# A hybrid attention layer on one Trainium2 core: one more pair of query tiles is searched beside attention

## The chip, the cores and the metric

The kernel runs on one core of a Trainium2 chip. The metric is the device time of one execution in microseconds (us). Every input and output lies in HBM; inside the core work runs on TensorE (PE, with its weight loads PEld), VectorE (DVE), ScalarE (ACT), GpSimd (POOL) and SyncE (SP, which issues all DMAs here). Each engine works through its own list of instructions in the order in which it was written, and waits at semaphores for the others.

## The reference

The layer takes 2048 tokens of width 1024, puts 16 meta tokens in front and computes

- `proj = h @ w_in`, split into queries, keys and values of branch A, queries and latents (`c_kv`) of branch B, the indexer's queries, key and head weights, and 2048 gate columns;
- branch A: chunk-causal sliding-window attention, 8 heads;
- branch B: for each query an index score over all visible keys, the sum over 8 heads of `w * relu(q_idx . k_idx)`; the best 256 keys are kept (`lax.top_k(score, 256)`), and attention runs over those alone;
- the gated sum of both branches, an output projection, a layer norm, a SwiGLU FFN and a second layer norm.

In float32, to float32 accuracy: products of the projection use three passes of a high and a low part (`matmul3`).

## The kernel before, in words

Queries are worked in 16 tiles of 128 rows (`TILES`); tile t sees `width(t) = 16 + 128 (t + 1)` keys, so tiles 12, 13, 14, 15 see 1680, 1808, 1936 and 2064. The kernel is four blocks, each ending with all engines:

1. `ln`: layer norm and the first eight column chunks of the projection.
2. `se` (the "second block"): in steps n = -39 to 106, three kinds of work side by side. (a) The rest of the projection: 96 units (a chunk of 128 columns for a group of 512 tokens), each of 8 *pieces*, a piece being one `matmul3` of 512 columns, three matmuls. (b) Index scores, one head of one tile in each step: step n has head m = n + 32, tile m // 8 (`IDX_AHEAD`). TensorE makes them (`index`, L845/L846; it runs two steps ahead), ScalarE rectifies them into three buffers (`rectify`, L920), VectorE adds them up (`sum_index`, L1033). (c) The search for the 256th largest score of a pair of tiles q = (2q, 2q+1), by bisection in 31 rounds (`ROUNDS`), and then the selection. The search of the even tile counts on VectorE (`tally`, L1054), that of the odd one on ScalarE (`tally`, L941/L943/L945: from round 9 on ScalarE makes the next candidate itself); GpSimd decides between rounds (`judge`). Two rounds of each go into a step. The even tile of pair q + 1 is searched in steps 16q - 8 to 16q + 7, the odd one in 16q to 16q + 15. Then each tile is selected in eight steps (`select`: `restore`, `mark_above`, `mark_equal`, `number_equal`, `choose`, `join`, `mask`) and its distances are stored in HBM (`distances`, `store_distances`). Pairs 0 to 6 (tiles 0 to 13, `LATE = 7`) are done so; tiles 12 and 13 are searched in steps 72 to 95 and selected in steps 88 to 103.
3. `at` (attention): one head of one tile per step, n = 0 to 127, tile n // 8. TensorE makes logits (L102 to L104), transposes (L1597, L1630) and weighs (L1619); VectorE adds distances to the logits (L1832); ScalarE takes exponentials (L1704, L1712) and copies transposed blocks out (L1724). Pair 7 (tiles 14 and 15), whose index scores stay in SBUF (`late_score`), is searched here, one round per step, in steps 56 to 89 (`search`, `LATE_STEP`): VectorE L1947, ScalarE L1764/L1766/L1768, GpSimd L1478. Tiles 14 and 15 are selected in steps 104 to 119, straight into the distance buffer.
4. `ff`: gates, output projection, FFN.

How many pieces of the projection a step of the second block takes is planned by `piece_steps`: it spreads them by an estimate of each step's other work (`columns`), never more than 8 in a step, and pauses for three steps where the second half of the token groups is swapped in (`RELOAD_STEPS`). The plan of before gives 8 pieces to each step from 55 to 102 (4 to 8 to most steps from 8 to 51), pauses at 52 to 54, and puts none at 103 to 106. Steps 96 to 102 hold 56 pieces and no index score: the last index score is added at step 95.

On every engine the order within a step is written out. TensorE's is: first block of the index score, half of the pieces, the other blocks, the other pieces. `index` waits until ScalarE has emptied the bank that it writes (two banks); `rectify` waits for VectorE to have used a buffer (`rel_free`).

The attention's search puts its work at the end of each engine's step:

```
def search(n):                       # of ScalarE, before
    r = n - LATE_STEP - 1
    if r == -1: orient()
    if r == 0: flip()
    if 0 <= r < ROUNDS: tally(r)
```

Of the kernel before, what the change touches and what calls it, by code (L numbers as in the profile page):

```python
# [62 lines left out]
LATE = TILES // 2 - 1  # L63
LATE_STEP = 7 * HEADS
FIRST_STEP, LAST_STEP = -IDX_AHEAD - 7, HEADS * (2 * LATE - 2) + 10
# [117 lines left out]
def project_and_select(nc, x, meta_tokens, ln0_g, ln0_b, w_in, b_gate, kv_norm_g, k_idx_g, k_idx_b, h0, proj, v_nat, h_kept, c_kept, dist_kept, late_score, w_uk, wuk_t):  # L183
# [6 lines left out]
    with Scope(nc, "pj") as s:  # L190
# [18 lines left out]
        with Scope(nc, "ln") as a:  # L209
            xt = [a.sb(f"x{u}", [P, D]) for u in range(2)]  # L210
            spare = [late_score[:, c // 2, c % 2 * D:c % 2 * D + D].rearrange("p (k c) -> p k c", k=KT) for c in range(4)]
            raws = [t[:, :, :] for t in raw] + spare + [a.sb(f"raw{c}", [P, KT, P])[:, :, :] for c in range(6, len(FIRST_CHUNKS))]
# [9 lines left out]
            part = [a.sb(f"part{v}", [P, GROUP]) for v in range(3)]  # L222
# [247 lines left out]
        with Scope(nc, "se") as a:  # L470
# [15 lines left out]
            score = [a.sb("score0", [P, 2, L - 2 * P]), late_score]  # L486
# [66 lines left out]
            with nc.Block() as block:  # L553
# [92 lines left out]
                def _(pool):  # L646
# [120 lines left out]
                    def part_b(n, half):  # L767
                        q, r = search_b(n, half)
                        if n >= 0 and n % (2 * HEADS) == 0 and half == 0 and n:
# [431 lines left out]
def attention(nc, proj, v_nat, wuk_t, w_uv, sinks, attn, c_kept, dist_kept, score):  # L1201
# [4 lines left out]
    with Scope(nc, "at") as s:  # L1206
# [22 lines left out]
        kth, fix_count, fix_cand = s.sb("kth", [P, 2]), s.sb("fix_count", [P, 1]), s.sb("fix_cand", [P, 1])  # L1229
# [80 lines left out]
        def late(t):  # L1310
            return score[:, t % 2, 0:width(t)]
# [7 lines left out]
        with nc.Block() as block:  # L1319
# [70 lines left out]
            def _(pool):  # L1390
# [42 lines left out]
                def orient(c):  # L1433
                    w = width(2 * LATE + c)
                    pool.wait_ge(count_ready[c], 1 + START)
# [14 lines left out]
                def judge(c, r):  # L1450
                    if c and len(EXPONENTS) < r < ROUNDS - 1:
                        return
                    pool.wait_ge(count_ready[c], 2 + r + START)
# [16 lines left out]
                    elif c:  # L1470
# [4 lines left out]
                        pool.tensor_tensor(one(kth, c), one(cand, c), one(step, c), ALU.add)  # L1475
                    else:
# [8 lines left out]
                        else:  # L1485
                            pool.tensor_tensor(one(kth, c), one(base, c), one(step, c), ALU.add)
                    pool.drain()

                def settle_a():
                    pool.tensor_scalar(one(undo, 0), one(sign, 0), 1.0, None, ALU.mult)  # L1490
                    pool.tensor_tensor(one(kth, 0), one(kth, 0), one(sign, 0), ALU.mult)
# [3 lines left out]
                def settle_first():  # L1495
                    pool.tensor_scalar(one(undo, 1), one(sign, 1), 1.0, None, ALU.mult)
                    pool.tensor_scalar(one(kth, 1), one(kth, 1), -1.0, None, ALU.mult)
                    pool.drain()
                    pool.tensor_tensor(fix_cand[:, :], one(kth, 1), steps[:, 1, MANTISSA - 1:MANTISSA], ALU.subtract).then_inc(fix_ready, 1)
                    w = width(2 * LATE + 1)  # L1500
# [3 lines left out]
                def settle_second():  # L1504
                    pool.wait_ge(fix_counted, 1 + START)
                    pool.tensor_scalar(one(step, 1), fix_count[:, :], one(wanted, 1), steps[:, 1, MANTISSA - 1:MANTISSA], ALU.is_ge, ALU.mult)
                    pool.drain()
                    pool.tensor_tensor(one(kth, 1), one(kth, 1), one(step, 1), ALU.subtract)
                    pool.drain()
                    pool.tensor_tensor(one(kth, 1), one(kth, 1), one(sign, 1), ALU.mult).then_inc(kth_ready[1], 1)  # L1510
                    pool.drain()

                def search(n):

                    r = n - LATE_STEP - 1
                    if r == -1:
                        orient(0)
                        orient(1)
                    if 0 <= r < ROUNDS:
                        judge(0, r)  # L1520
                        judge(1, r)
                    if r == ROUNDS - 1:
                        settle_a()
                        settle_first()
                    if r == ROUNDS + 1:
                        settle_second()
# [168 lines left out]
            def _(act):  # L1695
# [51 lines left out]
                def orient():  # L1747
                    t = 2 * LATE + 1
                    act.activation(junk_s[:, 0:width(t)], late(t), ACT.Sign, accum_out=one(count, 1)).then_inc(count_ready[1], 1)

                def flip():
                    t = 2 * LATE + 1
                    act.wait_ge(sign_ready[1], 1 + START)
# [3 lines left out]
                def tally(r):  # L1757

                    t, i = 2 * LATE + 1, r - len(EXPONENTS) - 1
                    if i <= 0:  # L1760
                        act.wait_ge(cand_ready[1], r + 1 + START)
# [8 lines left out]
                def search(n):  # L1770

                    r = n - LATE_STEP - 1
# [4 lines left out]
                    if 0 <= r < ROUNDS:  # L1777
                        tally(r)
# [39 lines left out]
            def _(dve):  # L1818
# [52 lines left out]
                def restore(t):  # L1871
                    c, x = t % 2, late(t)
                    dve.wait_ge(kth_ready[c], 1 + START)
                    dve.tensor_scalar(x, x, one(undo, c), None, ALU.mult)
                    dve.drain()

                def mark_above(t):
                    c, w, x = t % 2, width(t), late(t)
                    dve.tensor_scalar(greater[:, 0:w], x, one(kth, c), None, ALU.is_gt, ALU.add, accum_out=one(above, c))
                    dve.drain()  # L1880

                def mark_equal(t):
                    c, w, x = t % 2, width(t), late(t)
                    dve.tensor_scalar(equal[:, 0:w], x, one(kth, c), None, ALU.is_equal)
# [50 lines left out]
                def orient():  # L1935
                    t = 2 * LATE
                    dve.tensor_scalar(junk_v[:, 0:width(t)], late(t), 0.0, None, ALU.is_ge, ALU.add, accum_out=one(count, 0)).then_inc(count_ready[0], 1)

                def flip():
                    dve.wait_ge(sign_ready[0], 1 + START)  # L1940
                    dve.tensor_scalar(late(2 * LATE), late(2 * LATE), one(sign, 0), None, ALU.mult)
# [656 lines left out]
```

## Time and profile before

| | us |
|---|---|
| median of 3 runs | 4093.33 |
| lowest and highest | 4085.76, 4095.21 |
| the profiled execution | 4090.23 |
| its span, first to last instruction | 4088.1 |

| stretch of the span (us) | what runs |
|---|---|
| 0 to about 263 | first block |
| about 263 to 1209 | second block (last piece at 1205) |
| 1209 to about 2140 | attention |
| 2140 to 4088 | mixing and FFN |

In the span TensorE is busy 3731.0 us (91%), VectorE 1617.5 (40%), ScalarE 1777.7 (43%), GpSimd 1627.7 (40%). A busy TensorE counts modelled ends of matmuls that overlap; what it waits for is seen in the idle time before an instruction. The column PEclk is the clock that TensorE was granted, as a share of 2.4 GHz; it has two levels, 1.2 and 2.4 GHz.

### The profile page before, as it was taken

What the parts mean: (1) busy time and instruction counts of PE and PEld (TensorE: products, weight loads), DVE (VectorE), ACT (ScalarE), POOL (GpSimd) and SP (SyncE); (2) the same over time, 40 slices, a digit from 0 to 9 for tenths busy, and PEclk for the clock granted to TensorE, in tenths of its full rate; (3) what the DMA queues carried; (4) which work ended last, traced back from release to release, by engine and by line L of the source; (5) the groups of instructions that cost most, each with busy time, mean ns of one, the idle gap of its engine ahead of it and who ended that gap; (6) DMA issues with size and microseconds to landing.
All of it is one profiled execution on the core that took longest, in us unless ns stands there. A gap on an engine that the chain in (4) does not pass through costs nothing. (4 is left out here: it accounts for less than half of the span.)

```text
span 4088.1 us, 53536 instructions
## 1 busy us (share of the span) xinstructions
PE 3731.0 (91%) x18658; PEld 3092.7 (76%) x18658; DVE 1617.5 (40%) x2432; ACT 1777.7 (43%) x3161; POOL 1627.7 (40%) x1743
## 2 busy tenths in 40 slices
PE   5997788788889999999998989799999999999997
PEld 4875556566667888999986777688878878887886
DVE  4216666788732236634524665311131031113102
ACT  3213677778843668865542222222222222222221
POOL 5213566666521112110014555344444444444443
PEclk9988899899996999999998999899999999999999
DMA  7323322422231111110006565233333333333332
GB/s 232 141 73 94 81 65 64 154 64 85 64 108 39 44 44 31 43 35 23 15 10 203 201 204 182 67 108 97 135 113 97 124 103 114 98 138 112 94 98 83
DMA packets 421781, 396.38 MB, mean 97 GB/s; under 512 B 20424, under 2 KB 361624, under 8 KB 418232
## 3 DMA queue, kind: packets, MB, share of 16 engines
q1 hardware_dynamic: 410048, 342.28, 27.4%
q10 hardware_dynamic: 11520, 51.38, 3.4%
q8 instruction: 119, 1.95, 0.2%
q14 instruction: 94, 0.77, 0.1%
HBM read 302.51 MB, written 91.08 MB: 96 GB/s over the span
## 5 line engine op out<-in xcount | busy, mean ns | idle before, releaser
L2149 POOL TENSOR_TENSOR ff_w_lo<-ff_raw,ff_w_hi 128x1024 fp32r<-128x1024 f32 x328 | 787.0, 2400 | 958.3 <-ACT ff_w_hi L2187 958.3
L2187 ACT ACTIVATE ff_w_hi<-ff_raw 128x1024 fp32r<-128x1024 f32 x328 | 346.0, 1056 | 854.8 <-PE ff_bank L104 739.1
L102 PE MATMUL ff_bank<-ff_h_hi,ff_w_lo 128*128 128x512 f32 x1408 | 551.2, 392 | 16.3 <-POOL ff_w_lo L2149 10.3
L103 PE MATMUL ff_bank<-ff_h_hi,ff_w_hi 128*128 128x512 f32 x1408 | 550.0, 391 | 0.0
L104 PE MATMUL ff_bank<-ff_h_lo,ff_w_hi 128*128 128x512 f32 x1408 | 550.0, 391 | 0.0
L102 PE MATMUL ff_bank<-ff_w_hi,ff_f 128*128 128x512 f32 x960 | 373.9, 389 | 4.6 <-DVE ff_mixed L2434 4.3
L104 PE MATMUL ff_bank<-ff_w_lo,ff_f 128*128 128x512 f32 x960 | 373.5, 389 | 0.0
L103 PE MATMUL ff_bank<-ff_w_hi,ff_f 128*128 128x512 f32 x960 | 373.5, 389 | 0.0
L1619 PE MATMUL at_ctx<-at_p_t,at_c_nat 128*128 128x128 f32 (+1 forms) x2432 | 351.5, 285 | 7.9 <-ACT at_ctx_t L1730 7.0
L1619 PEld LDWEIGHTS at_ctx<-at_p_t,at_c_nat 128*128 128x128 f32 (+1 forms) x2432 | 306.1, 194 | 37.7 <-ACT at_ctx_t L1730 13.2
L1724 ACT ACTIVATE at_p_t<-at_turn 128x512 f32<-128x512 f32 (+4 forms) x416 | 214.2, 544 | 266.3 <-PE at_turn L1597 226.4
L102 PEld LDWEIGHTS ff_bank<-ff_h_hi,ff_w_lo 128*128 128x128 f32 x1408 | 265.7, 189 | 75.0 <-issue 20.2
L103 PEld LDWEIGHTS ff_bank<-ff_h_hi,ff_w_hi 128*128 128x128 f32 x1408 | 265.9, 189 | 55.3
L104 PEld LDWEIGHTS ff_bank<-ff_h_lo,ff_w_hi 128*128 128x128 f32 x1408 | 265.6, 189 | 55.7
L845 PE MATMUL se_big_i<-se_ki_hi,se_qi 128*128 128x512 f32 (+16 forms) x392 | 149.7, 382 | 155.2 <-ACT se_rel L920 154.1
L2285 ACT ACTIVATE ff_f<-ff_mixed 128x512 f32 (+1 forms) x88 | 55.6, 632 | 437.3 <-DVE ff_mixed L2434 437.3
L845 PEld LDWEIGHTS se_big_i<-se_ki_hi,se_qi 128*128 128x128 f32 x392 | 79.3, 202 | 217.6 <-ACT se_rel L920 187.6
L102 PEld LDWEIGHTS ff_bank<-ff_w_hi,ff_f 128*128 128x128 f32 x960 | 180.2, 188 | 43.9 <-issue 6.6
L104 PEld LDWEIGHTS ff_bank<-ff_w_lo,ff_f 128*128 128x128 f32 x960 | 180.2, 188 | 37.6
L103 PEld LDWEIGHTS ff_bank<-ff_w_hi,ff_f 128*128 128x128 f32 x960 | 180.2, 188 | 37.2
L920 ACT ACTIVATE se_rel<-se_big_i 128x272 f32<-128x272 f32 (+14 forms) x248 | 155.5, 632 | 90.5 <-DVE late_score L1033 47.8
L1832 DVE CUSTOM_DVE_ANT_0 at_u_b<-at_big_l,at_dist 128x528 f32<-128x528 f32 (+11 forms) x128 | 106.8, 834 | 207.9 <-PE at_big_l L104 198.8
(350 smaller groups left out, 7740.8 us busy)
## 6 DMA issues: line engine op xcount, KB each, us to landing
ff_raw<-in_w_ff_gate SPq DMA_DIRECT2D x88, 512.0 KB, 3.8
ff_raw<-in_w_ff_up SPq DMA_DIRECT2D x88, 512.0 KB, 3.8
ff_raw<-in_w_ff_down SPq DMA_DIRECT2D x88, 512.0 KB, 3.5
pj_raw<-in_w_in SPq DMA_DIRECT2D x50, 512.0 KB, 4.6
proj<-se_row SPq DMA_DIRECT2D x96, 256.0 KB, 2.2
ff_f<-proj SPq DMA_DIRECT2D x64, 256.0 KB, 3.5
ff_raw<-in_w_out SPq DMA_DIRECT2D x32, 512.0 KB, 3.5
ln_x<-in_x SPq DMA_DIRECT2D x16, 512.0 KB, 4.9
```

The lines of the kernel that those rows point to most:

```text
L102: pe.matmul(out, lhs_lo, rhs_hi, start=start, stop=False)
L103: pe.matmul(out, lhs_hi, rhs_hi, start=False, stop=False)
L104: return pe.matmul(out, lhs_hi, rhs_lo, start=False, stop=stop)
L845: pe.matmul(big_i[i % 2][:, a:a + n], qi_2[t % 2][:, h, :], ki_hi[:, cols], start=True, stop=False)
L920: act.activation(rel[i % RELS][:, 0:wb], big_i[i % 2][:, 0:wb], ACT.Relu).then_inc(rel_ready, 1)
L1619: last = pe.matmul(ctx[:, 0, :], c_nat[0:rows, a:a + P], p_t[v][0:rows, m, :], start=(a == 0), stop=(a + rows == w))
L1724: act.activation(p_t[v][0:rows, 0:many, :], turn[u][0:rows, 0:many * P].rearrange("p (m q) -> p m q", m=many), ACT.Copy).then_inc(turn_fre ...
L1832: dve.tensor_tensor_reduce(u_b[n % 3][:, a0:a0 + wb], big_l[i % 2][:, 0:wb], dist[t % 2][:, a0:a0 + wb], 2.0 ** -(h + 1), min_b[:, c, b - ...
L2149: pool.tensor_tensor(w_lo[u][:, :], raw[u][:, :], f32(w_hi[u][:, :]), ALU.subtract).then_inc(lo_ready[u], 1)
L2187: act.activation(w_hi[u][:, :], raw[u][:, :], ACT.Copy).then_inc(hi_ready[u], 1)
L2285: act.activation(piece(f_hi, 2 * i + n), feature[:, :], ACT.Copy).then_inc(feat_hi, 1)
```

## The change

`LATE` goes from 7 to 6: the second block searches and selects tiles 0 to 11 only. The scores of tiles 12 and 13 stay in SBUF too (`late_score` is now both score buffers, and some scratch of the first block is laid into them), and the attention block has two searches: pair 6 from step 37, pair 7 from step 71 (it was 56). Tiles 12 and 13 are selected in attention's steps 88 to 103, with pair 7's search running. Attention loads distances for tiles 0 to 11 only. The counts write to scratch tiles of their own (`junk_v`, `junk_s`) instead of `greater` and `equal`.

The second block ends at step 97 instead of 106. `piece_steps` is unchanged but gives another plan: the 56 pieces of steps 96 to 102 go to earlier steps, 45 more to steps -32 to 39 and 11 more to steps 40 to 55; the pause is at steps 45 to 47 instead of 52 to 54; steps 56 to 95 hold 8 pieces each as before.

```diff
-LATE = TILES // 2 - 1
-LATE_STEP = 7 * HEADS
-FIRST_STEP, LAST_STEP = -IDX_AHEAD - 7, HEADS * (2 * LATE - 2) + 10
+LATE = TILES // 2 - 2
+LATE_STEPS = {LATE: 37, LATE + 1: 71}
+FIRST_STEP, LAST_STEP = -IDX_AHEAD - 7, max(HEADS * (2 * LATE - 2) + 10, STEPS - IDX_AHEAD + 1)
...
-            score = [a.sb("score0", [P, 2, L - 2 * P]), late_score]
+            score = late_score
...
-        junk_v, junk_s = greater, equal
-        undo = s.sb("undo", [P, 2])
+        junk_v, junk_s = s.sb("junk_v", [P, L], BF16), s.sb("junk_s", [P, L], BF16)
+        undo = s.sb("undo", [P, 4])
...
         def late(t):
-            return score[:, t % 2, 0:width(t)]
+            return score[t // 2 % 2][:, t % 2, 0:width(t)]
+
+        def late_round(n):
+
+            for q, first in LATE_STEPS.items():
+                if first <= n <= first + ROUNDS + 2:
+                    return q, n - first - 1
+            return None, None
+
+        def nth(q, many):
+
+            return (q - LATE) * many + START
...
                 def search(n):
 
-                    r = n - LATE_STEP - 1
+                    q, r = late_round(n)
                     if r == -1:
-                        orient()
+                        orient(q)
                     if r == 0:
-                        flip()
-                    if 0 <= r < ROUNDS:
-                        tally(r)
+                        flip(q)
+                    if q and 0 <= r < ROUNDS:
+                        tally(q, r)
...
-        late_score = s.sb("score", [P, 2, L])
+        late_score = [s.sb("score0", [P, 2, L - 2 * P]), s.sb("score1", [P, 2, L])]
```

The other hunks carry the pair q through `orient`, `flip`, `tally`, `judge`, `settle_*` and `restore` of the three engines, with semaphore counts and thresholds (`kth`, `undo`) for both pairs.

## Rows read from the trace of the kernel before

**Rows 1.** The page's head and its part 1, busy time of each engine.

```profile
span 4088.1 us, 53536 instructions
PE 3731.0 (91%) x18658; PEld 3092.7 (76%) x18658; DVE 1617.5 (40%) x2432; ACT 1777.7 (43%) x3161; POOL 1627.7 (40%) x1743
```

**Rows 2.** Windows, second block: length, PE, PEld, DVE, ACT, POOL busy, PEclk, DMA, GB/s.

```profile
625.00:683.00 58.00, 50.62 (x209) 38.86 (x208) 37.25 (x61) 42.69 (x75) 39.12 (x89) 0.91 0.24 70
683.00:744.00 61.00, 52.10 (x231) 40.28 (x230) 50.67 (x67) 47.28 (x86) 36.47 (x72) 0.98 0.30 81
744.00:808.00 64.00, 45.76 (x172) 34.92 (x172) 48.58 (x61) 49.88 (x78) 42.54 (x86) 0.78 0.56 194
808.00:873.00 65.00, 57.99 (x258) 45.62 (x257) 55.50 (x64) 51.39 (x86) 39.77 (x66) 1.00 0.25 75
...
945.00:1021.00 76.00, 61.97 (x260) 47.20 (x259) 66.20 (x65) 59.60 (x90) 47.57 (x75) 1.00 0.26 72
1021.00:1105.00 84.00, 68.83 (x265) 53.68 (x264) 64.89 (x65) 64.17 (x84) 53.68 (x91) 0.90 0.23 66
1105.00:1167.00 62.00, 58.10 (x262) 46.78 (x262) 32.91 (x33) 55.63 (x87) 15.68 (x22) 1.00 0.23 74
1167.00:1206.00 39.00, 38.93 (x167) 31.02 (x165) 15.85 (x12) 6.52 (x10) 13.98 (x13) 1.00 0.24 85
```

**Rows 3.** Waits of TensorE, 1021 to 1105 us: total us, times, longest.

```profile
PE se_big_i L845 <- ACT se_rel L920: 15.2, 8, 3.9
```

**Rows 4.** Waits of TensorE, 1105 to 1167 us.

```profile
PE se_big_i L845 <- ACT se_rel L920: 3.9, 6, 1.1
```

**Rows 5.** Groups by line, VectorE, 942 to 1105 us: busy, mean ns, idle before.

```profile
L1054 DVE TENSOR_SCALAR_CACHE_REDUCE se_junk_v<-se_score,se_cand 128x1680 bf16<-128x1680 f32 x31 | 60.8, 1962 | 20.8 <-POOL se_cand L726 15.5 <-POOL se_cand L703 2.4 <-POOL se_cand L714 1.7
```

**Rows 6.** Groups by line, ScalarE, 1019 to 1167 us.

```profile
L945 ACT ACTIVATE se_junk_s<-se_score,se_cand 128x1808 bf16<-128x1808 f32 x31 | 55.9, 1803 | 15.4 <-POOL se_cand L703 9.7 <-POOL se_cand L714 4.1
...
L943 ACT ACTIVATE se_cand<-se_verdict,se_cand,se_steps 128x1 f32<-128x1 f32 x22 | 8.5, 387 | 1.8 <-issue 0.3
L941 ACT ACTIVATE se_verdict<-se_count,se_limit 128x1 f32<-128x1 f32 x22 | 6.5, 295 | 1.8
```

**Rows 7.** Windows, attention: the columns of rows 2, eight steps in each stretch.

```profile
1393.00:1434.00 41.00, 40.71 (x301) 35.69 (x303) 13.40 (x26) 25.52 (x68) 6.86 (x7) 1.00 0.16 46
1434.00:1478.00 44.00, 43.84 (x323) 38.97 (x321) 14.47 (x26) 26.94 (x67) 6.58 (x7) 1.00 0.15 44
1478.00:1527.00 49.00, 48.84 (x361) 43.62 (x360) 17.68 (x34) 30.83 (x71) 6.75 (x14) 1.00 0.14 41
1527.00:1583.00 56.00, 55.10 (x407) 48.31 (x406) 36.66 (x59) 48.59 (x93) 16.39 (x42) 1.00 0.12 37
1583.00:1642.00 59.00, 58.75 (x442) 52.90 (x442) 36.53 (x58) 52.73 (x105) 14.99 (x37) 1.00 0.12 37
1642.00:1704.00 62.00, 61.86 (x469) 56.22 (x469) 37.65 (x58) 55.49 (x108) 12.59 (x30) 1.00 0.12 36
1704.00:1770.00 66.00, 65.89 (x502) 60.09 (x501) 39.40 (x59) 54.61 (x106) 15.29 (x39) 1.00 0.11 35
1770.00:1839.00 69.00, 68.27 (x515) 62.55 (x514) 22.49 (x43) 38.40 (x83) 6.62 (x6) 1.00 0.11 34
```

**Rows 8.** Timeline of ScalarE, 1601 to 1605 us, one round: start, us.

```profile
1601.61 0.29 ACT L1764 ACTIVATE at_verdict<-at_count,at_limit 128x1 f32<-128x1 f32 x1
1601.97 0.39 ACT L1766 ACTIVATE at_cand<-at_verdict,at_cand,at_steps 128x1 f32<-128x1 f32 x1
1602.42 2.02 ACT L1768 ACTIVATE at_equal<-late_score,at_cand 128x2064 bf16<-128x2064 f32 x1
...
1604.44 1.06 ACT L1724 ACTIVATE at_p_t<-at_turn 128x512 f32<-128x512 f32 x2
```

**Rows 9.** Groups by line, VectorE, 1478 to 2080 us.

```profile
L1947 DVE TENSOR_SCALAR_CACHE_REDUCE at_greater<-late_score,at_cand 128x1936 bf16<-128x1936 f32 x31 | 69.0, 2225 | 2.5 <-issue 2.4
...
L1890 DVE TENSOR_TENSOR_SCAN late_score<-at_equal 128x1936 f32<-128x1936 bf16 (+1 forms) x2 | 8.6, 4314 | 0.0
```

More of the change, by code:

```diff
@@ L221, in project_and_select @@
             rstd = [a.sb(f"rstd{u}", [P, 1]) for u in range(2)]
-            part = [a.sb(f"part{v}", [P, GROUP]) for v in range(3)]
+            part = [late_score[0][:, c, D:D + GROUP] for c in range(2)] + [wuk_t[:, :, :].rearrange("p j c -> p (j c)")]
             zeros = part[0]
@@ L768, in part_b @@
                         q, r = search_b(n, half)
-                        if n >= 0 and n % (2 * HEADS) == 0 and half == 0 and n:
+                        if n > 0 and n % (2 * HEADS) == 0 and half == 0 and n // (2 * HEADS) < LATE:
                             settle_second(n // (2 * HEADS))
@@ L1474, in judge @@
                         pool.drain()
-                        pool.tensor_tensor(one(kth, c), one(cand, c), one(step, c), ALU.add)
+                        pool.tensor_tensor(one(kth, k_of(c, q)), one(cand, c), one(step, c), ALU.add)
                     else:
@@ L1485, in judge, with settle_a @@
                         else:
-                            pool.tensor_tensor(one(kth, c), one(base, c), one(step, c), ALU.add)
+                            pool.tensor_tensor(one(kth, k_of(c, q)), one(base, c), one(step, c), ALU.add)
                     pool.drain()
-                def settle_a():
-                    pool.tensor_scalar(one(undo, 0), one(sign, 0), 1.0, None, ALU.mult)
-                    pool.tensor_tensor(one(kth, 0), one(kth, 0), one(sign, 0), ALU.mult)
+                def settle_a(q):
+                    pool.tensor_scalar(one(undo, k_of(0, q)), one(sign, 0), 1.0, None, ALU.mult)
+                    pool.tensor_tensor(one(kth, k_of(0, q)), one(kth, k_of(0, q)), one(sign, 0), ALU.mult)
@@ L1878, in mark_above @@
                     c, w, x = t % 2, width(t), late(t)
-                    dve.tensor_scalar(greater[:, 0:w], x, one(kth, c), None, ALU.is_gt, ALU.add, accum_out=one(above, c))
+                    dve.tensor_scalar(greater[:, 0:w], x, one(kth, k_of(c, t // 2)), None, ALU.is_gt, ALU.add, accum_out=one(above, c))
                     dve.drain()
@@ L1933, in distances, with orient, flip @@
                     dve.drain()
-                def orient():
-                    t = 2 * LATE
+                def orient(q):
+                    t = 2 * q
                     dve.tensor_scalar(junk_v[:, 0:width(t)], late(t), 0.0, None, ALU.is_ge, ALU.add, accum_out=one(count, 0)).then_inc(count_ready[0], 1)
-                def flip():
-                    dve.wait_ge(sign_ready[0], 1 + START)
-                    dve.tensor_scalar(late(2 * LATE), late(2 * LATE), one(sign, 0), None, ALU.mult)
+                def flip(q):
+                    dve.wait_ge(sign_ready[0], 1 + nth(q, 1))
+                    dve.tensor_scalar(late(2 * q), late(2 * q), one(sign, 0), None, ALU.mult)
@@ L1942, in flip, with tally, tally_fix @@
                     dve.drain()
[L1944 to L1946 removed]
+                def tally(q, r):
+                    t = 2 * q
+                    dve.wait_ge(cand_ready[0], r + 1 + nth(q, ROUNDS))
                     dve.tensor_scalar(junk_v[:, 0:width(t)], late(t), one(cand, 0), None, ALU.is_ge, ALU.add,
                                       accum_out=one(count, 0)).then_inc(count_ready[0], 1)
[L1950 to L1953 removed]
+                def tally_fix(q):
+                    t = 2 * q + 1
+                    dve.wait_ge(fix_ready, 1 + nth(q, 1))
+                    dve.tensor_scalar(junk_v[:, 0:width(t)], late(t), fix_cand[:, :], None, ALU.is_ge, ALU.add,
@@ L1954, in tally_fix @@
                                       accum_out=fix_count[:, :]).then_inc(fix_counted, 1)
                 def search(n):
-                    r, (t, h) = n - LATE_STEP - 1, divmod(n, HEADS)
+                    (q, r), (t, h) = late_round(n), divmod(n, HEADS)
                     if r == -1:
-                        orient()
+                        orient(q)
                     if r == 0:
-                        flip()
-                    if 0 <= r < ROUNDS:
-                        tally(r)
+                        flip(q)
@@ L1965, in search @@
+                    if q and 0 <= r < ROUNDS:
+                        tally(q, r)
                     if r == ROUNDS:
-                        tally_fix()
+                        tally_fix(q)
                     if t + 1 >= 2 * LATE and t + 1 < TILES:
```

83 lines of the change are left out of this document (39 added, 44 removed).

## The prediction, made before the changed kernel was run

> **What bounds the kernel now.** I read the page's part 1 first: TensorE is busy 91% of the span, VectorE, ScalarE and GpSimd 40 to 43% [rows 1]. But that is an average over four blocks, and the change touches two of them, which the windows tell apart. In the second block I cut the span wherever TensorE had done the pieces of eight more steps of the plan, so a row of that table is eight steps [rows 2]. In the last row (steps 96 to 102, projection alone) TensorE is busy 38.93 of 39 us: 167 matmuls, 0.233 us each, so a piece of three costs 0.70 us and 56 pieces 39.2 us. In the rows before it TensorE has slack: 61.97 of 76 us busy in steps 72 to 79, 68.83 of 84 in steps 80 to 87, then 58.10 of 62 in steps 88 to 95. The difference between these three is the search: two searches run in the first two, only ScalarE's in the third. TensorE's waits say the same: in the 84 us it stood 15.2 us until ScalarE had emptied an index bank, in the 62 us only 3.9 [rows 3, 4]. ScalarE and VectorE come late with the index score because a round of the search stands before it in their lists.
>
> In attention the same columns look different [rows 7]: TensorE is busy 40.7 of 41 to 68.3 of 69 us in every row, at PEclk 1.00. This block is bound by TensorE's own work, and the search of pair 7 (steps 56 to 89, from the fourth row on) lies beside it. ScalarE there is busy 48.59 of 56, 52.73 of 59 and 55.49 of 62: 87 to 90%.
>
> **The change, part by part.** The sum is against the profiled execution's 4090.2 us (its span 4088.1 and 2.1 around it); the median of the runs is 3.1 us more.
>
> *The tail goes.* Steps 96 to 102 disappear from the end of the block. VectorE's share there (selection of tile 13) is hidden anyway; what the path loses is the 39.2 us of pieces: **-39**. What follows the last piece (copy out, store, end of block) stays.
>
> *Steps 80 to 95 without search.* TensorE's own work in a step is 8 pieces, 5.6 us, and the index score. With 512 columns in 0.233 us (0.455 ns a column) and two passes over the keys this is 2 x 1936 x 0.455 = 1.76 us for tile 14 and 1.88 for tile 15. TensorE is two steps ahead, so steps 80 to 87 hold six heads of tile 14 and two of tile 15: 44.8 + 14.3 = 59.1 us. Now 84. VectorE loses 16 rounds of 1.96 us [rows 5], ScalarE 16 of about 2.7 (1.80 + 0.39 + 0.30 and the reading of the sum) [rows 6]. What is left for VectorE is adding and selecting tile 11, far under 59. I add 1.5 us of waits: 60.6, **-23**. Steps 88 to 95 hold the last six heads of tile 15: 44.8 + 11.3 = 56.1; with 1 us of waits 57, now 62: **-5**.
>
> *Steps 72 to 79 without VectorE's search.* ScalarE's search of pair 5 stays. The row to compare is steps 88 to 95 of before, which has just that: 62 us for 56.1 of TensorE's work, 5.7 more. TensorE's work here is 44.8 + six heads of tile 13 (1.65 each) + two of tile 14 = 58.2; plus 5.7 is 63.9, now 76: **-12**.
>
> *The 56 pieces moved forward.* As work of TensorE they cost 39.2 us, in steps where TensorE has idle time. Bounds: 0 and +39. The nearest rows are steps 32 to 63: 48, 55, 36 and 64 pieces take 58, 61, 64 and 65 us [rows 2]. The row with 20 to 28 pieces fewer than its neighbours is no shorter than the line between them (63), so up to there a row is set by the search and index chain, and a piece is nearly free. The pause for the reload is in that row too, so it is not a clean proof. I take **+6**: some pieces will stand before an index score that ScalarE is ready for.
>
> A row that bears on the clock: the stretch with the pause was granted 0.78 of 2.4 GHz, that is it partly ran at the 1.2 GHz level, after TensorE had been without pieces; the dense rows around it got 0.98 and 1.00 [rows 2]. "TensorE: Matmul & The Clock Gate" of the Trainium skill (Part 1) says that the throttled state is the default and that activity releases it. By that rule the denser steps would run no slower, but a TensorE that waits on ScalarE in attention could fall to the lower level; no attention row shows this (1.00 with ScalarE at 90%).
>
> *Attention: pair 7's search moves from step 56 to 71.* Its rows there have more TensorE work per step (62 us and up per eight steps) and ScalarE at most at 90%: it becomes slightly better hidden. The rows grow by 3, 5, 7, 3, 3, 4, 3 us; the 7 where pair 7's search begins suggests that it cost 2 to 3 us. Half of it goes: **-1**.
>
> *Attention: pair 6's search in steps 37 to 70.* On ScalarE a round of pair 7 occupies 2.83 us from its first instruction to the next work [rows 8]. For 1808 columns instead of 2064 it is 0.21 less (1.803 against 2.016), 2.62; the first rounds have no verdict and candidate (0.81) and take 1.81. In steps 40 to 47: 26.94 + 7 x 1.81 + 2.62 = 42.2 us of work in a row of 44. In steps 48 to 55: 30.83 less the 2.1 of pair 7's first count, plus 8 x 2.62 = 49.7 us in a row of 49: **ScalarE is full there**. In steps 56 to 63, 30.8 (on the line between 26.94 and 38.40) + 21.0 = 51.8 of 55. So for some 16 steps TensorE will wait. If ScalarE reaches 95% of its time, the rows become 44.5 and 52.5: +0.5 and +3.5; the start (first count, sign flip and two rounds within steps 37 to 39, 41 us row) another +2; steps 56 to 70 +1. Sum **+7**. Bounds: 0 if all of it is hidden as at 90%, and +80 if none is: 31 x 1.99 + 22 x 0.68 + 4 us for count and flip is what ScalarE gets in addition.
>
> *VectorE in attention.* Pair 6's counts fall into rows where it is busy a third of the time. In steps 88 to 103 a step can hold a count (2.2) and the scan (4.3 at 1936 columns) [rows 9] beside its 2.7 of other work: up to 9.4 us against steps of 7.8 to 9, for two steps in a row. Its logits are two steps ahead of their use, so a lag of 3 us is covered: **+1**, up to +8 if not.
>
> *At no cost:* separate scratch for the counts, scores in other addresses (same shapes), two distance tiles fewer to store and load (DMA idle, nobody waits), semaphore arithmetic. GpSimd's rounds run once per step and wait for counts.
>
> Sum: -39 - 23 - 5 - 12 + 6 - 1 + 7 + 1 = -66; 4090.2 - 66 = **4024 us**.
>
> **Rivals.** (A) *All hidden*: the moved pieces and attention's search cost 0 to 2: 4090 - 79 = 4011. For it: the 36-piece row, and the 90% rows. Against: steps 48 to 55. (B) *The moved pieces are paid in full*: +33 on the forecast, 4057. For it: TensorE's list is in order, each piece delays the index score behind it. Against: 36 pieces took as long as 55. (C) *ScalarE becomes the bound of attention from step 37 to 63*, not only where its sum exceeds the row: transposes, copies and exponentials go back and forth between the two engines, and a tally between them costs half of its length in 26 rounds, 26 x 2.4 / 2 = 31 instead of 7: 4048. (D) *Slower*: the same place, but ScalarE's 80 us stand wholly in series with TensorE: 4024 - 7 + 80 = 4097. It decides from the point where at least 75 of the 80 us show up; in the 90% rows 3 or fewer of 80 did. (E) *Steps 72 to 95 don't speed up*, because the adding chain (rectify, three buffers, VectorE) bounds them rather than the rounds: 20 of the 40 us lost, 4044. Against: the 62 us row has the same adding and little waiting. (F) *The change doesn't do what it says*: if the searches' counts met late thresholds, GpSimd would stall selection; there is no sign of that, price unknown, around 4090.
>
> **How the numbers follow.** Forecast 55%, A 15%, B 8%, C 11%, E 6%, D 3%, F 2%. The forecast's own range is 4014 to 4034. Eight in ten need A and most of C and E: 4006 to 4049. A measurement here tells about 0.2% (8 us) from no change. Slower is D alone, 3%; same is F, 2%; faster 95%.
>
> **What would show it.** In the second block: the last piece at about 1205 - 73 = 1132 us; steps 72 to 95 in 182 us instead of 222; steps -32 to 55 as long as before within 10 us. If these grow by 30, B. In attention: rows of steps 40 to 55 longer by 4 us together with ScalarE over 93% busy; rows 88 to 103 unchanged; PEclk 1.00. C shows as rows 37 to 63 longer by 25 or more with ScalarE, not TensorE, without idle time. The prediction is wrong if steps 80 to 87 stay above 68 us, or if attention as a whole grows by over 20.

## The result and the profile after

| | before | changed |
|---|---|---|
| median of 4 runs, us | 4092.82 | 4016.35 |
| lowest and highest | 4085.76, 4095.21 | 4012.19, 4023.9 |
| the profiled execution, us (its span) | 4090.23 (4088.1) | 4023.9 (4021.7) |
| ratio of the changed kernel to before | | 0.9818, 95% interval [0.9807, 0.9829] |

The change takes 76 us off the median. The forecast was 4024, with 4006 to 4049 as its range. The profiled execution is the longest of the four, so the profile shows 66 of the 76 us.

The windows of the second block, cut again where TensorE had done the pieces of eight more steps (columns as in [rows 2]). The first four are steps 32 to 63, the last three steps 72 to 95, which are now the end of the block:

```profile
629.00:690.00 61.00, 53.82 (x238) 42.92 (x236) 41.00 (x63) 45.53 (x80) 41.78 (x92) 0.96 0.31 89
690.00:748.00 58.00, 42.56 (x182) 34.32 (x181) 48.22 (x63) 45.75 (x84) 37.70 (x71) 0.84 0.65 226
748.00:811.00 63.00, 59.64 (x259) 47.65 (x259) 49.42 (x63) 49.36 (x78) 41.89 (x86) 0.96 0.23 62
811.00:876.00 65.00, 58.45 (x259) 45.73 (x258) 55.28 (x66) 52.07 (x89) 43.62 (x74) 1.00 0.27 76
946.00:1010.00 64.00, 60.05 (x260) 47.61 (x259) 31.51 (x31) 58.59 (x90) 21.27 (x27) 1.00 0.29 84
1010.00:1069.00 59.00, 59.00 (x265) 48.40 (x263) 38.44 (x33) 25.75 (x32) 20.40 (x17) 1.00 0.34 108
1069.00:1125.00 56.00, 56.00 (x261) 46.00 (x260) 17.23 (x19) 20.66 (x29) 10.53 (x12) 1.00 0.14 48
```

Steps 72 to 95 took 76, 84 and 62 us [rows 2] and take 64, 59 and 56. In the last two TensorE is never idle, and the waits for ScalarE of [rows 3, 4] are gone; in steps 72 to 79, where ScalarE still searches pair 5, they are small:

```profile
PE se_big_i L845 <- ACT se_rel L920: 4.0, 5, 0.8
```

Step 72 begins at 946 us, as before (945), although 56 more pieces have been done by then. Step 40 begins 7 us later than before, and what lies between gives 6 us back. The last piece is issued at 1124.9 instead of 1205.1 us.

The same windows in attention, eight steps each, from step 32 to step 63 and from 88 to 103. Against [rows 7], which end with step 95, the first three (41, 44 and 49 us there) and that of steps 88 to 95 (69) have grown:

```profile
1311.00:1355.00 44.00, 42.13 (x299) 36.78 (x298) 22.32 (x35) 33.22 (x77) 11.83 (x27) 0.96 0.15 43
1355.00:1401.00 46.00, 44.85 (x329) 39.52 (x327) 29.59 (x42) 41.68 (x88) 17.10 (x44) 1.00 0.14 42
1401.00:1453.00 52.00, 49.81 (x364) 43.68 (x366) 30.72 (x48) 48.13 (x101) 12.61 (x30) 1.00 0.13 39
1453.00:1509.00 56.00, 54.82 (x404) 47.84 (x400) 33.47 (x58) 49.91 (x107) 12.61 (x30) 1.00 0.13 37
...
1695.00:1767.00 72.00, 69.62 (x517) 63.12 (x517) 54.11 (x71) 59.49 (x115) 19.96 (x30) 1.00 0.07 20
1767.00:1841.00 74.00, 72.61 (x540) 66.64 (x539) 53.35 (x69) 56.34 (x107) 22.49 (x36) 1.00 0.07 19
```

ScalarE is busy 48.13 of 52 us in steps 48 to 55, 93%, and TensorE is no longer busy throughout: 49.81 of 52. More finely, by ScalarE's copies of the context (one in each step), the stretches of 40.9, 44.2 and 49.4 us became 44.3, 45.4 and 52.1, and those of 69.4 and 73.1 us became 71.7 and 74.2. From the first of these copies to that of step 120 attention took 836.8 us and takes 846.7. A second profiled execution of the changed kernel took 848.6; the 1.9 us between the two lie in steps 8 to 15, long before the search. What follows took 2017.1 us from there to the end of the span and takes 2021.8, with the same code; that is unevenness between executions (2012.2 to 2022.8 us in all the profiled executions of this document). So -81.0 before attention, +9.9 in it and +4.7 behind it are the -66.4 of the span.

### The profile page after: what moved, and what is told of

The parts are those of the page before. It is cut to its first block and busy times, and to the rows that moved or that the text cites. A ratio compares the mean times of both kernels' runs of the same rounds, so it can differ in the third digit from the quotient of the medians.

```text
span 4021.7 us, 53531 instructions
## 1 busy us (share of the span) xinstructions
PE 3706.1 (92%) x18658; PEld 3080.0 (77%) x18658; DVE 1620.2 (40%) x2432; ACT 1772.5 (44%) x3161; POOL 1611.5 (40%) x1743
## 5 line engine op out<-in xcount | busy, mean ns | idle before, releaser
L2299 ACT ACTIVATE ff_f<-ff_mixed 128x512 f32 (+1 forms) x88 | 55.6, 632 | 438.8 <-DVE ff_mixed L2448 438.8
L1054 DVE TENSOR_SCALAR_CACHE_REDUCE se_junk_v<-late_score,se_cand 128x400 bf16<-128x400 f32 (+4 forms) x155 | 180.2, 1162 | 124.4 <-POOL se_cand L726 97.8
L1033 DVE SCALAR_TENSOR_TENSOR late_score<-se_rel,se_w_idx,late_score 128x272 f32<-128x272 f32 (+14 forms) x217 | 194.9, 898 | 73.1 <-ACT se_rel L920 66.1
L945 ACT ACTIVATE se_junk_s<-late_score,se_cand 128x528 bf16<-128x528 f32 (+4 forms) x155 | 180.2, 1163 | 66.5 <-POOL se_cand L703 41.5
```

The lines of the kernel that those rows point to most:

```text
L945: act.activation(junk_s[:, 0:width(t)], score_of(t), ACT.Sign, bias=one(cand, 1), accum_out=one(count, 1)).then_inc(count_ready[1], 1)
L1033: dve.scalar_tensor_tensor(out=out, in0=rel[i % RELS][:, 0:wb], scalar=w_idx[:, t, h:h + 1], in1=out, op0=ALU.mult, op1=ALU.add).then_inc( ...
L1054: dve.tensor_scalar(junk_v[:, 0:width(t)], score_of(t), one(cand, 0), None, ALU.is_ge, ALU.add, accum_out=one(count, 0)).then_inc(count_re ...
L2299: act.activation(piece(f_hi, 2 * i + n), feature[:, :], ACT.Copy).then_inc(feat_hi, 1)
```

## The experiments

Kernels with a ratio were timed in turn with the kernel before on one chip; two (without ScalarE's rounds of pair 6, without VectorE's rounds of pair 7) ran once only, with a profile, and have none. In the tables "attention" is from the context copy of step 0 to that of step 120 in the profiled execution, and the stretches are measured between such copies too.

### One part at a time: the plan of pieces, and the search

The search moved, the pieces planned as before:

```diff
-FIRST_STEP, LAST_STEP = -IDX_AHEAD - 7, max(HEADS * (2 * LATE - 2) + 10, STEPS - IDX_AHEAD + 1)
+FIRST_STEP, LAST_STEP = -IDX_AHEAD - 7, HEADS * (2 * (LATE + 1) - 2) + 10
...
-        tally = 2 * width(2 * q + 2) + 600 if 0 <= q < LATE - 1 else 0
-        chosen = [1, 2, 1, 2, 1, 1, 1, 0][h] * width(t + 1) if 0 < t < 2 * LATE - 1 else 0
+        tally = 2 * width(2 * q + 2) + 600 if 0 <= q < LATE else 0
+        chosen = [1, 2, 1, 2, 1, 1, 1, 0][h] * width(t + 1) if 0 < t < 2 * LATE + 1 else 0
```

> The changed kernel with the plan of pieces of the kernel before: 56 pieces in steps 96 to 102 again, the pause at steps 52 to 54. Everything else as changed. Theory: the tail of 39 us comes back, and the 1 to 6 us that the moved pieces cost go: 35 to 38 us slower than the changed kernel, about 4053, ratio to before 0.990; last piece about 40 us earlier than before the change. Rival (a piece moved is paid where it goes, in full or half): the plan is worth less than 20 us, ratio under 0.987.

And the kernel before with the new plan alone:

```diff
-def piece_steps():
+def piece_steps(LATE=TILES // 2 - 2, LAST_STEP=STEPS - IDX_AHEAD + 1):
```

> The kernel before with the new plan of pieces alone; pair 6 is searched and selected in the second block as before. Theory: steps up to 71 take as long as before within 2 us, steps 72 to 95 stay at 222 us, and the tail holds only the selection of tile 13 on VectorE (about 16 us of work) and the storing of its distances: some 20 us of the 39 are gained, about 4073, ratio 0.995. So the change is worth more than its parts, because each part empties the tail only halfway. Rival (the plan gives its whole 39 us by itself): 4054, ratio 0.990. Other rival (pieces paid in full where they go): 4092 or more.

| | ratio to before, 95% | step 40 begins | step 56 | step 72 | last piece | attention's first copy |
|---|---|---|---|---|---|---|
| before | 1 | 682.9 | 808.1 | 945.2 | 1205.1 | 1234.2 |
| new plan only | 0.9937 [0.9921, 0.9954] | 690.5 | 810.8 | 946.7 | 1162.1 | 1208.9 |
| search moved, old plan | 0.9913 [0.9897, 0.9930] | 683.7 | 809.2 | 946.1 | 1163.3 | 1191.6 |
| both (the change) | 0.9818 [0.9807, 0.9829] | 690.1 | 810.4 | 946.3 | 1124.9 | 1153.2 |

In the sum the moved pieces cost next to nothing: with either plan step 72 begins within 0.2 us of the other where the search of pair 6 has gone, within 1.5 where it has not. They are not free where they go, though. The new plan has 45 more of them before step 40, and step 40 begins 6.4 to 7.6 us later with it. That is 0.14 to 0.17 us for each, where a piece alone takes 0.70. Between steps 40 and 72, with 11 more, 6.1 to 6.2 us come back. The plans differ there in the place of the pause too: steps 48 to 55 took 64.2 and 64.4 us with 36 pieces and the pause, 62.7 (twice) with 64 pieces and no pause; steps 40 to 47 took 61.1 us (twice) with 55 pieces, 57.7 (twice) with 38 pieces and the pause. No run moves the pause alone. Of the theories, full or half payment falls; the plan is worth 38.4 us at attention's start. With the search moved and the old plan the tail is back, TensorE alone, and the stretches before it are as short as in the changed kernel. Columns as in [rows 2]:

```profile
1009.00:1068.00 59.00, 59.00 (x264) 48.41 (x263) 39.24 (x33) 25.59 (x32) 26.89 (x20) 1.00 0.30 91
1068.00:1125.00 57.00, 57.00 (x266) 46.77 (x265) 17.22 (x19) 21.86 (x31) 13.35 (x16) 1.00 0.23 69
1125.00:1164.00 39.00, 39.00 (x168) 31.21 (x166) 0.00 (x0) 6.66 (x9) 5.63 (x8) 1.00 0.18 61
```

The new plan alone gives 25 us at attention's start, where 20 was expected: the last piece comes 43 us earlier, but attention starts 47 us after it instead of 29, because the selection of tile 13 now stands there with nothing beside it. This is the timeline of VectorE there (start, us), with the last piece issued at 1162.1:

```profile
1163.77 1.16 DVE L1066 TENSOR_SCALAR se_score<-se_score,se_undo 128x1808 f32<-128x1808 f32 x1 [1.18 <-POOL se_kth L755]
...
1168.51 3.93 DVE L1082 TENSOR_TENSOR_SCAN se_score<-se_equal 128x1808 f32<-128x1808 bf16 x1
...
1176.80 2.04 DVE L1147 SCALAR_TENSOR_TENSOR se_dist<-se_query_key,se_equal 128x1808 f32<-128x1808 f32 x1
```

One thing came otherwise than expected: steps 72 to 95 did not stay at 222 us but took 216 (73, 81 and 62), which is why the last piece comes 43 us earlier and not 39. No run shows why.

25.3 and 42.6 us add to 67.9; together they bring 81.0. The tail held two things side by side, and only taking both out removes it.

### Pair 6's rounds taken out of attention

The first count, the flip and the rounds of pair 6 are left out, first on all three engines, then ScalarE's alone; and, for the last stretches, VectorE's rounds of pair 7. With `LEFT_OUT` as `[(6, 0), (6, 1)]`, `[(6, 1)]` and `[(7, 0)]` (pair, tile of the pair). The first hunk is ScalarE's, the second GpSimd's; VectorE's is like them, and the semaphore thresholds follow:

```diff
                     q, r = late_round(n)
+                    if (q, 1) in LEFT_OUT:
+                        return
                     if r == -1:
                         orient(q)
...
-                        orient(q, 0)
-                        orient(q, 1)
+                        for c in range(2):
+                            if (q, c) not in LEFT_OUT:
+                                orient(q, c)
```

> The changed kernel without the first count, the flip and the 31 rounds of pair 6 in attention, on VectorE, ScalarE and GpSimd (tiles 12 and 13 are still selected, against a threshold that was never searched). Theory (those rounds fill ScalarE in steps 37 to 63): the attention stretches of steps 32 to 55, 44.3, 45.4 and 52.1 us in the changed kernel, fall to about 41, 44 and 48; attention is shorter by 7 to 8 us and the whole by as much, about 4008 us, ratio to before 0.980. The stretches of steps 88 to 103 (71.7 and 74.2 us) stay, because selection and pair 7's rounds are still there. Rival (the growth of attention is an unevenness between executions, or comes from the scores' new addresses): stretches stay at 44, 45 and 52, ratio 0.982.

> The changed kernel without ScalarE's part of pair 6's rounds in attention (tile 13's search left out); VectorE's and GpSimd's rounds for tile 12 stay. Theory (ScalarE is what is full): steps 32 to 55 take about 41, 44 and 48 us as without any rounds. Rival (VectorE's count stands before the logits that TensorE and ScalarE wait for): they stay at 44, 45 and 52, or lose less than half of the excess of 7 us.

> The changed kernel without VectorE's part of pair 7's rounds (tile 14's search left out). Theory: steps 88 to 103 fall from 71.7 and 74.2 us to 69.5 and 73.1, as in the kernel before, since VectorE no longer falls behind in a tile's steps 1 to 3; steps 72 to 87 stay. Rival (ScalarE's rounds of pair 7 do it): they stay at 71.7 and 74.2.

| steps | 32-39 | 40-47 | 48-55 | 56-63 | 88-95 | 96-103 | attention |
|---|---|---|---|---|---|---|---|
| before | 40.9 | 44.2 | 49.4 | 55.6 | 69.4 | 73.1 | 836.8 |
| changed | 44.3 | 45.4 | 52.1 | 56.1 | 71.7 | 74.2 | 846.7 |
| the same, again | 44.3 | 45.4 | 52.1 | 56.1 | 71.7 | 74.1 | 848.6 |
| no rounds of pair 6 | 40.9 | 44.2 | 49.3 | 54.9 | 71.7 | 74.2 | 838.7 |
| none on ScalarE | 40.9 | 44.9 | 49.4 | 54.9 | 71.7 | 74.1 | 840.5 |
| none on VectorE, pair 7 | 42.7 | 45.4 | 52.1 | 56.1 | 70.3 | 73.2 | 841.7 |

The kernel without any rounds of pair 6 was timed: ratio 0.9805 [0.9788, 0.9821], which is not told apart from the changed kernel's 0.9818 (4014 us, where 4008 was expected); the stretches do tell. Their growth repeats to 0.1 us and vanishes with the rounds. Nearly all of it in steps 32 to 63 is ScalarE's: without its part, VectorE's counts cost 0.7 us in steps 40 to 47 and nothing elsewhere. One size was off: the rounds cost 8.6 us in the four stretches from step 32 to 63, and the start alone 3.4 of them, where I had put 2. In steps 88 to 103 the excess over before is 3.4 us, and 2.3 of it go with VectorE's rounds of pair 7; the expectation had all of it go.

ScalarE's timeline at the start (step 38 of the changed kernel; start, us) shows flip and first count back to back, 3.7 us, and the windows show what TensorE does meanwhile:

```profile
1339.16 1.81 ACT L1768 ACTIVATE late_score<-late_score,at_sign 128x1808 f32<-128x1808 f32 x1
1341.04 1.80 ACT L1782 ACTIVATE at_junk_s<-late_score,at_cand 128x1808 bf16<-128x1808 f32 x1
...
1342.84 0.58 ACT L1738 ACTIVATE at_p_t<-at_turn 128x512 f32<-128x512 f32 x1
```

```profile
1331.00:1339.00 8.00, 8.00 (x63) 7.38 (x63) 5.77 (x8) 7.78 (x21) 2.50 (x9) 1.00 0.01 3
1339.00:1347.00 8.00, 6.42 (x38) 5.67 (x37) 3.28 (x6) 7.93 (x13) 3.53 (x8) 0.80 0.00 0
```

TensorE waits 1.6 us, and in the same 8 us its granted clock is 0.80, that is partly at the 1.2 GHz level. "TensorE: Matmul & The Clock Gate" of the Trainium skill (Part 1) says that the throttled state is the default and that activity releases it. A fall right behind a wait agrees with that (0.80 here, 1.00 in the 8 us before); it is the fall that the prediction named and had not seen in [rows 7]. It goes with half of the excess of this stretch: the kernel without VectorE's rounds of pair 7 (table above) and the kernel with both edits (below) have the same wait in the same place and no fall, and take 42.7 us for it, not 44.3. So the two long instructions by themselves cost 1.8 us, close to the 2 of the forecast.

### An earlier start

```diff
-LATE_STEPS = {LATE: 37, LATE + 1: 71}
+LATE_STEPS = {LATE: 21, LATE + 1: 71}
```

> The changed kernel with pair 6's search started at attention's step 21 instead of 37, all else the same. Theory (a stretch is as long as the longer of TensorE's work and ScalarE's sum, which it fills to about 95%): ScalarE's sums are 20.4 + 5 rounds in steps 16 to 23 (hidden), 23.1 + 8 x 1.8 = 38 of 38.5 in steps 24 to 31, 25.4 + 8 x 2.6 = 46.4 against 41 in steps 32 to 39, 27.0 + 21 = 48 against 44 in steps 40 to 47, 29 + 7 x 2.6 = 47 against 49.3 in steps 48 to 55. At 95% that is 40, 49, 50.5 and 50: about 19 us over the stretches without rounds, where the start at 37 costs 8. So 10 to 12 us slower than the changed kernel, ratio 0.985 to 0.987. Rival (a round costs the same wherever it stands, 31 rounds for 8 us): no difference. Rival D (what exceeds comes wholly in series): 40 us and more slower.

Ratio 0.9855 [0.9831, 0.9880]; attention 862.9 us, 14 to 16 more than in the changed kernel. Windows from step 16 on, eight steps each:

```profile
1240.00:1283.00 43.00, 38.12 (x241) 32.89 (x239) 20.28 (x35) 29.35 (x71) 12.32 (x27) 0.88 0.14 40
1283.00:1325.00 42.00, 38.90 (x281) 32.62 (x278) 27.56 (x43) 37.87 (x89) 16.46 (x43) 1.00 0.15 43
1325.00:1371.00 46.00, 42.30 (x297) 36.60 (x297) 28.45 (x42) 43.53 (x98) 12.62 (x30) 0.96 0.15 41
1371.00:1420.00 49.00, 46.37 (x327) 40.51 (x325) 29.60 (x42) 46.23 (x101) 12.62 (x30) 0.97 0.14 39
```

The price depends on where the rounds stand, as expected, and neither rival holds: 31 rounds cost 23 us here (steps 16 to 63) and 9 there, not the same and not 40 more. The two stretches from step 32 came out under their sums (46.5 and 48.5 us measured, 49 and 50.5 expected), although each has a fall of the clock in it (0.96 and 0.97). ScalarE did fill them to 94 to 95%, as the theory said; its work was put 2 to 3 us too high. But steps 16 to 23, which should have hidden their five rounds, took 42.8 instead of 35.7 us with ScalarE at 68%: flip and first count fall into one short step there, and the clock of 0.88 over 43 us is by itself worth about 5 of the 7 us (an estimate: 0.12 x 43). An average over eight steps does not see one step that is too full.

### Less work on ScalarE, and VectorE's work spread

GpSimd makes the odd tile's next candidate in all rounds (the hunk is ScalarE's; GpSimd's `judge` gets three small instructions per round for it):

```diff
                 def tally(q, r):
...
-                    if i <= 0:
-                        act.wait_ge(cand_ready[1], r + 1 + nth(q, len(EXPONENTS) + 2))
-                    else:
-                        act.drain()
-                        act.activation(verdict[:, :], one(count, 1), ACT.Sign, bias=limit[:, :])
-                        act.drain()
-                        act.activation(one(cand, 1), verdict[:, :], ACT.Identity, scale=steps[:, 1, i:i + 1], bias=one(cand, 1))
-                        act.drain()
+                    act.wait_ge(cand_ready[1], r + 1 + nth(q, ROUNDS))
```

Selection starts one step earlier:

```diff
-                    if (at, half) == (1, 0):
-                        restore(t)
-                    if (at, half) == (1, 1):
-                        mark_above(t)
+                    if (at, half) == (7, 0) and t + 1 < TILES:
+                        restore(t + 1)
+                        mark_above(t + 1)
...
+                    if t + 1 == 2 * LATE - 1 and h == 7:
+                        select(t + 1, h, 0)
```

> The changed kernel as it is, once more, as the mark for the three kernels below on one chip: ratio to before 0.981 to 0.983; attention stretches of steps 32 to 55 near 44, 45 and 52 us, of steps 88 to 103 near 71.7 and 74.2 us.

> The changed kernel with ScalarE's two small instructions per round from round 9 on (verdict and candidate, 0.8 us of its time) given to GpSimd in attention. Theory (ScalarE's sum against the stretch is what makes steps 40 to 63 longer): ScalarE's load in steps 48 to 55 falls from 49.7 to about 43.5 us of 48, so that stretch falls from 52.1 to about 50, steps 56 to 63 from 56.1 to 55, steps 40 to 47 hardly (one such round there); 3 us in all. Rival C (each count stands between TensorE and ScalarE wherever the sum is): the stretches stay within 1 us, since the count of 1.8 us is unchanged. Other rival: GpSimd's answer comes too late for ScalarE's next count, and the stretches grow.

> The changed kernel with restore and mark_above of attention's selection moved from a tile's step 1 to step 7 of the tile before, where VectorE has nothing to select. Theory (in steps 88 to 103 VectorE falls behind at steps 1 to 3 of a tile, and TensorE waits for its low part of the absorbed query): the stretches 71.7 and 74.2 us fall to about 69.5 and 73.2, 3 us in all; the whole is 3 us faster, which these rounds hardly tell. Rival (pair 7's rounds on ScalarE make these stretches longer): they stay.

> Both edits together. Theory: the gains add, about 6 us under the changed kernel, ratio to before 0.980 to 0.981. Rival: what one stretch gives is lost in the next, ratio as that of the changed kernel.

In later runs, the flip in a step of its own as well:

```diff
-LATE_STEPS = {LATE: 37, LATE + 1: 71}
+LATE_STEPS = {LATE: 35, LATE + 1: 70}
...
-                    return q, n - first - 1
+                    return q, {0: -1, 1: -0.5}.get(n - first, n - first - 2)
...
-                    if r == 0:
+                    if r == -0.5:
                         flip(q)
```

> Both edits of the kernel before this one (selection spread, GpSimd's verdict), and the sign flip of a tile gets a step of its own before the first round, so that pair 6 starts at step 35 and pair 7 at 70. Theory (flip and first count together, 3.8 us of ScalarE in one step, make TensorE wait 1.6 us at step 39, and in some executions its clock falls to 1.2 GHz for a stretch after that wait): the stretch of steps 32 to 39 falls from 42.7 (without the fall) or 44.3 us (with it) to 41.5 or less, and no fall is seen in it. In the whole 1 to 2 us, which these rounds can't tell. Rival (what costs there is the answer of GpSimd that ScalarE waits for): the stretch stays at 42.7 or 44.3.

> The kernel with both edits (selection spread, GpSimd's verdict) once more, beside the one with the flip apart: ratio to before 0.980 to 0.982, 1 to 2 us more than that one, not told apart.

| | ratio to before, 95% | 32-39 | 40-47 | 48-55 | 56-63 | 88-95 | 96-103 | attention |
|---|---|---|---|---|---|---|---|---|
| changed, again | 0.9834 [0.9821, 0.9847] | 44.3 | 45.4 | 52.1 | 56.1 | 71.7 | 74.1 | 848.6 |
| selection spread | 0.9826 [0.9813, 0.9839] | 44.3 | 45.4 | 52.1 | 56.2 | 70.3 | 73.2 | 844.4 |
| GpSimd's verdict | 0.9821 [0.9808, 0.9834] | 44.3 | 45.4 | 49.6 | 54.9 | 70.9 | 74.2 | 843.6 |
| both | 0.9808 [0.9794, 0.9821] | 42.7 | 45.4 | 49.6 | 54.9 | 69.4 | 73.1 | 838.7 |
| both, second time | 0.9813 [0.9800, 0.9827] | 42.7 | 45.4 | 49.6 | 54.9 | 69.4 | 73.1 | 838.4 |
| both and flip apart | 0.9811 [0.9797, 0.9824] | 42.4 | 45.4 | 49.6 | 54.9 | 69.5 | 73.1 | 838.1 |

Taking 0.8 us from a round gives steps 48 to 55 back 2.5 of their 2.8 us, although the count of 1.8 us still stands where it stood: so it is the sum of ScalarE's work against the stretch that costs, not the place of the count (rival C). The window of steps 48 to 55 with GpSimd's verdict has TensorE busy throughout again and ScalarE at 86%:

```profile
1403.00:1453.00 50.00, 49.71 (x369) 44.05 (x369) 30.57 (x48) 43.00 (x87) 18.61 (x55) 1.00 0.14 40
```

Spreading the selection gives 2.3 us, the same as leaving VectorE's rounds of pair 7 out. GpSimd's verdict takes another 0.8 us out of steps 88 to 95, where pair 7's rounds lie on ScalarE too, and with both edits steps 88 to 103 are back at the 69.4 and 73.1 us of before. So the rival that blamed ScalarE's rounds of pair 7 holds for about a quarter of the 3.4 us. With both edits attention is as long as without pair 6's rounds at all (838.7). Than the changed kernel measured beside them, both edits are faster by 4024.1 - 4015.1 = 9 us; the intervals of the ratios only touch, but no run of the one reaches the other (4009.4 to 4016.3 against 4019.4 to 4025.8 us). The flip apart missed: 42.4 us instead of 41.5 or less. The burst is gone, but the very first count now falls into step 35, the tile's shortest, which takes 5.6 us instead of the 3.7 of before. No fall of the clock is seen there; as the kernel with both edits had none either, that says nothing for the flip. Its gain, if there is one, isn't told by the times.

## Why the prediction was right

The forecast of 4024 us was the profiled execution's own 4023.9, which is in part luck; against the median it was 8 us high, inside its own range of 4014 to 4034. Term by term:

| step of the sum | forecast | measured |
|---|---|---|
| tail of 56 pieces | -39 | -39 (1125 to 1164 in the old-plan kernel) |
| steps 80 to 87 | -23 | -25 |
| steps 88 to 95 | -5 | -6 |
| steps 72 to 79 | -12 | -12 |
| pieces moved forward | +6 | +1 |
| attention, rounds on ScalarE (less pair 7's move) | +6 | +7 |
| attention, VectorE in steps 88 to 103 | +1 | +3 |
| behind attention | 0 | +5 in this execution |

*The second block.* What let the three stretches be sized to 2 us was that TensorE's own work could be added up from two durations in a row where it was alone (0.233 us for 512 columns), and that a stretch with one search instead of two stood in the trace of before. The forecast of 63.9 us for steps 72 to 79 came from that stretch and met 64. Two small slips stand in the working and change nothing: 62 less 56.1 is 5.9 us and not 5.7, and the row of 36 pieces has 19 to 28 fewer than its neighbours, not 20 to 28.

*The moved pieces.* This is the mis-sized term: 6 us charged, 0.2 and 1.5 us measured between the two plans. The charge was about what the pieces cost up to step 40 (6.4 and 7.6 us); that the steps behind give it back was not in the sum. The row with 36 pieces, on which the idea of a free piece rested, was no fair witness: the same steps are 1.5 us shorter with 64 pieces and the pause elsewhere.

*Attention.* The place (steps 37 to 55, ScalarE full) and the sign were right, with 52.1 us measured for 52.5 forecast in steps 48 to 55. The start was under-sized: 3.4 us for 2, of which 1.6 go with the fall of the clock that the forecast had named and put at nothing. "PEclk 1.00", one of its signs, failed with that (0.96 over steps 32 to 39). So did "rows 88 to 103 unchanged": VectorE's lag was not covered as I had argued. Its low part of the absorbed query (`at_ql_lo`) came late for TensorE once in each of the two tiles. My check of the slack had looked at the logits alone. TensorE's weight loads in steps 88 to 103 of the changed kernel show the waits (total, times, longest); in the same stretches of the kernel with the selection spread there are none:

```profile
PEld at_misc L1568 <- DVE at_ql_lo L1854: 2.8, 2, 1.6
```

*The errors cancelled in part.* The second block gave 8 us more than forecast, attention cost 3 more, and the unchanged last block happened to be 5 longer in that execution. The sum met the profile to 0.1 us; the terms did not, and that they added up so well is luck.

Of the rivals, A (all hidden, 4011) was nearest to the median for half of a reason: the moved pieces cost 1 us in the sum, attention's rounds were not hidden. B and E are refuted by the windows, C by its own size (25 us or more in steps 37 to 63, measured 9) and by the kernel with GpSimd's verdict, D by attention's 10 us against 80, and F by the block that ended 80 us earlier.

## What to carry to other kernels

Where an in-order engine waits for others, more work of its own costs less than its length (45 pieces, 31 us of work, delayed step 40 by 6 to 8 us here): sum that work per stretch from a row in which it runs alone, and take the stretch's length against that. A tail that holds two kinds of work side by side pays only once both are gone (25 and 43 us apart, 81 together here). When work moves beside a saturated engine, add up the *helper's* time per step and not only per stretch: at 89 to 91% the rounds cost 1.2 us in stretches of 45 and 56, at 93% 2.8 us in 52, and two long instructions in one short step cost 1.8 us, or 3.4 with the fall of the clock.

## What the runs showed of the hardware

TensorE's granted clock fell to the 1.2 GHz level in attention after a single wait of 1.6 us in an otherwise full stretch, and not always. The kernel with both edits has the same instructions of ScalarE at that place and the same busy time of TensorE as the changed kernel, whose window is shown above (6.42 of 8 us, clock 0.80); its own window of the same 8 us:

```profile
1339.00:1347.00 8.00, 6.42 (x48) 5.66 (x47) 3.99 (x7) 7.93 (x14) 3.30 (x8) 1.00 0.00 0
```

The fall costs 1.6 us here. In the eight profiled executions with this start five had it (changed twice, old plan, selection spread, GpSimd's verdict) and three had not (without VectorE's rounds of pair 7, both edits twice). The wait alone does not decide. In the same five the clock had also fallen for a moment at step 18, long before the search, and in the three it had not, although TensorE's waits there (1.1 and 0.9 us) are the same in all of them and in the kernel before. The changed kernel, then the kernel with both edits:

```profile
1244.00:1252.00 8.00, 7.07 (x38) 5.56 (x36) 1.86 (x5) 4.25 (x14) 1.04 (x1) 0.79 0.33 90
```

```profile
1244.00:1252.00 8.00, 6.80 (x46) 5.60 (x47) 2.39 (x9) 3.75 (x12) 1.04 (x1) 1.00 0.33 90
```

Steps 16 to 23 took 36.8 to 36.9 us with that fall and 35.7 without. The kernel without ScalarE's rounds of pair 6 fell at step 18 too, and not at step 38, where it has no wait. The two kernels that were profiled twice did the same both times; what decides was not found out.

A longer fall stands at attention's start in every execution, and [rows 7] begin behind it, so "no attention row shows this" in the prediction holds for its own rows alone. In the kernel before, TensorE did nothing for 9 us between its last piece (1205) and attention's first work; the clock fell in that gap and stayed at the 1.2 GHz level until 1301; the first row is that kernel, the second the changed one:

```profile
1209.00:1301.00 92.00, 73.43 (x289) 59.80 (x290) 21.78 (x68) 27.32 (x89) 12.98 (x61) 0.50 0.24 71
```

```profile
1129.00:1204.00 75.00, 59.47 (x237) 48.79 (x238) 17.66 (x58) 21.26 (x70) 11.93 (x60) 0.50 0.27 78
```

How long it lasts differs between executions. In the other profiled execution of the changed kernel it lasted 92 us, as in the kernel before, and steps 8 to 15 took 39.7 us and not 37.9: that is the 1.9 us between the two.

A GpSimd instruction on one column took 1.02 us in the second block of the kernel before and 0.37 us in attention, in that kernel (0.367) as in the changed one (0.369), for the same operation of the search:

```profile
L723 POOL TENSOR_SCALAR se_step<-se_count,se_wanted,se_steps 128x1 f32<-128x1 f32 x23 | 23.4, 1020 | 22.5 <-DVE se_junk_v L1054 22.0 <-issue 0.6
```

```profile
L1492 POOL TENSOR_SCALAR at_step<-at_count,at_wanted,at_steps 128x1 f32<-128x1 f32 x19 | 7.0, 369 | 81.5 <-DVE at_junk_v L1961 81.3 <-issue 0.2
```

Spans on GpSimd are rough, and no run was made to find the cause, so it stays open; nobody waited for the difference in attention.
